# Causal masks of two attention branches moved off TensorE: a kept-at-one scan, GpSimd on the diagonal blocks

## The reference, cut to what matters

```python
# branch A, stick-breaking, strictly causal (s < t)
z = einsum("bhqd,bhkd->bhqk", q, k) * 128 ** -0.5
log_keep = where(mask, log_sigmoid(-z), 0.0)
between = cumsum(log_keep, reverse=True) - log_keep
w = where(mask, exp(log_sigmoid(z) + between), 0.0)
# branch B, forgetting attention, causal (s <= t)
logits = z + cum_q[..., :, None] - cum_k[..., None, :]
p = softmax(where(s <= t, logits, -inf))
```

## Time and profile before

| | |
|---|---|
| median of 3 runs | 3790.38 us (3785.99 to 3910.45) |
| the profiled execution | 3785.02 us |
| its span on the slowest core (core 0) | 3783.5 us |
| spans of the 8 cores | 3759.2 to 3783.5 us |
| branch A, from the first scan to the last product | 107.0 to 595.7 us of the span |
| branch B, from the first addition to the last scaling | 595.7 to 1065.8 us |
| mask products | 256 |

### The profile page before, as it was taken

One profiled execution on the slowest core, in us unless ns is written; L12 is line 12 of the kernel. 1 busy time (PEld: TensorE's weight loads), 2 busy tenths in 40 slices (PEclk: granted clock), 3 DMA queues, 4 the chain that ended last, 5 costly groups with the idle time before them and its releaser, 6 DMA issues.

```text
span 3783.5 us, 56865 instructions; the slowest of 8 cores (3759.2 to 3783.5 us)
## 1 busy us (share of the span) xinstructions
PE 3683.0 (97%) x21124; PEld 1837.0 (49%) x21124; DVE 1738.2 (46%) x1692; ACT 1140.3 (30%) x1796; POOL 348.3 (9%) x467
## 2 busy tenths in 40 slices
PE   7999999999889999999999999999999999999999
PEld 6555656656534444444444444444444444444444
DVE  5788888887833333334333333332222322322233
ACT  5667777877731112222121111110001000000001
POOL 1000000000021112112110000000000000000001
PEclk9999999999999999999999999999999999999999
DMA  7565656767774467778895556556665565455568
GB/s 252 131 151 132 141 139 147 163 156 153 164 214 167 140 200 236 231 239 264 237 263 192 190 193 235 195 182 205 206 198 189 188 223 181 176 206 205 178 221 268
DMA packets 422367, 733.03 MB, mean 194 GB/s; under 512 B 333120, under 2 KB 333504, under 8 KB 352592
## 3 DMA queue, kind: packets, MB, share of 16 engines
q1 hardware_dynamic: 380048, 509.11, 45.1%
q0 software_dynamic: 40896, 216.10, 18.7%
q10 hardware_dynamic: 1152, 4.19, 0.3%
HBM read 567.77 MB, written 81.85 MB: 172 GB/s over the span
## 4 chain that ended last, share of the span: by engine, by line
PE 82%; DVE 7%; DMA 6%; issue 3%; ACT 1%; SPq 0%; POOL 0%; DVEq 0%; ACTq 0%; POOLq 0%
PE ps L78 82%; DVE Pr L78 5%; DMA WT<-W 2%; DMA xb<-x 1%; DVE W L78 1%; DMA OT<-OTs 1%; DMA mixs<-ost 1%; DMA xs<-x 1%; ACT W L78 0%; SPq L78 0%; DVE lg L78 0%; DVE wbf L78 0%; ACT kp L78 0%; DVE hb L78 0%; DVE ost L78 0%
## 5 line engine op out<-in xcount | busy, mean ns | idle before, releaser
L78 PE MATMUL ps<-u2T,wbf 128*128 128x512 bf16 x5632 | 1215.9, 379 | 0.0
L78 PE MATMUL ps<-uT,wbf 128*128 128x512 bf16 (+1 forms) x4480 | 940.6, 363 | 13.1 <-ACT sg L78 6.5
L78 PEld LDWEIGHTS ps<-u2T,wbf 128*128 128x128 bf16 x5632 | 551.1, 98 | 664.5
L78 DVE CAST wbf<-wst 128x2048 bf16<-128x2048 f32 x426 | 528.0, 1264 | 515.3 <-PE ps L78 429.3
L78 PEld LDWEIGHTS ps<-uT,wbf 128*128 128x128 bf16 x4480 | 416.1, 99 | 458.9 <-issue 20.5
L78 PE MATMUL ps<-wbf,aT 128*128 128x512 bf16 x2464 | 532.1, 379 | 0.0
L78 ACT ACTIVATE sg<-ps 128x512 f32<-128x512 f32 x264 | 155.0, 597 | 1234.3 <-PE ps L78 1214.2
L78 DVE TENSOR_TENSOR aT<-ps,sg 128x512 bf16<-128x512 f32 x176 | 121.6, 691 | 762.7 <-PE ps L78 759.7
L78 PEld LDWEIGHTS ps<-wbf,aT 128*128 128x128 bf16 x2464 | 241.1, 98 | 290.7
L78 DVE TENSOR_TENSOR_SCAN Pr<-kp 128x2047 bf16<-128x2047 f32 (+15 forms) x128 | 310.0, 2422 | 34.2 <-ACT kp L78 25.0
L78 ACT ACTIVATE junk<-ps 128x512 bf16<-128x512 f32 x128 | 76.5, 598 | 782.0 <-DVE ost L78 744.0
(11 more groups left out here) (96 smaller groups left out, 2039.9 us busy)
## 6 DMA issues: line engine op xcount, KB each, us to landing
wst<-wfg_t SPq DMA_DIRECT2D x88, 1024.0 KB, 7.3
wst<-wfu_t SPq DMA_DIRECT2D x88, 1024.0 KB, 5.4
wst<-wfd_t SPq DMA_DIRECT2D x88, 1024.0 KB, 5.8
wst<-wg_t SPq DMA_DIRECT2D x56, 1024.0 KB, 8.0
wst<-wqkv_t POOLq DMA_DIRECT2D x42, 1024.0 KB, 7.0
wst<-wo_t SPq DMA_DIRECT2D x32, 1024.0 KB, 7.9
wst<-wb_t SPq DMA_DIRECT2D x30, 1024.0 KB, 8.4
xs<-x SPq DMA_DIRECT2D x16, 1024.0 KB, 11.7
```

The costliest lines, as they stand in the source:

```text
L78: ins = getattr(eng, meth)(**kw)
```

## The change

- The mask product in `Zp` goes, in both branches, and with it the reading of `cbf` by the scores.
- Branch A, the product: the scan becomes state = max(state * kp, U), where `U` is a row pattern (`Um`, bfloat16, 128 x 2048) that is 0 everywhere but in the last 128 columns, and there 1 on the masked elements (s >= t within the block). The factor is below one, so a masked position keeps the state at one. `Um` lies in the memory of the second `Llo` tile, is written once by GpSimd ahead of the heads, and is read with its end laid at the row's end.
- Branch A, the weight: GpSimd multiplies the diagonal block of `W` by a 0/1 tile (`low_bf`), in place, after the sigmoid of the piece that has the block and before VectorE's product.
- Branch B: GpSimd adds `mfx_bf` (0 and -1e30) onto the 128 columns of `Lhi` or `Llo` that belong to the next row's diagonal block, in place (`mask_next`). The call stands behind VectorE's addition of the row's first piece where i > 8 and behind that of its last piece otherwise; after row 0 it is done for row 15 of the next head. The rows come in falling order, so a block that was lowered is not read again in that head.
- The first load of the second `Llo` tile moves from the early part of branch A to the start of branch B, since `Um` lies there.

```diff
@@ _emit @@
-    msb_bf = cbf.t[:, 0:128]
+    low_bf = cbf.t[:, 0:128]
+    upp_bf = cbf.t[:, 384:512]
...
+    Um, Umr = fx["Llo"][1].view([128, S], BF16), fx["Llo"][1].r
+    kb.op(POOL, "memset", dict(ap=Um[:, 0:S - 128], constant=0.0), writes=[Umr])
+    kb.op(POOL, "tensor_copy", dict(out=Um[:, S - 128:S], in_=upp_bf), reads=[cbf.r], writes=[Umr])
...
+    def mask_next(h, i):
+        L = fx["Lhi"] if i >= 8 else fx["Llo"][h % 2]
+        blk = L.t[:, (i % 8) * 128:(i % 8 + 1) * 128]
+        kb.op(POOL, "tensor_tensor", dict(out=blk, in0=blk, in1=mfx_bf, op=ALU.add), reads=[cbf.r], writes=[L.r])
@@ Zp @@
-            dg = e == 128 * (i + 1)
...
-            if dg:
-                calls.append(("matmul", dict(out=t[:, e - 128 - a:e - a], lhsT=ident_bf, rhs=msb_bf if hx < NH else mfx_bf,
-                                             start=False, stop=True, skip_group_check=True)))
-        kb.group(PE, calls, reads=[qT.r, kT.r, cbf.r], writes=rs)
+        kb.group(PE, calls, reads=[qT.r, kT.r], writes=rs)
@@ X_sb @@
+        if b == n:
+            kb.op(POOL, "tensor_tensor", dict(out=w_.t[:, n - 128:n], in0=w_.t[:, n - 128:n], in1=low_bf, op=ALU.mult),
+                  reads=[cbf.r], writes=[wh[1 if a else 0]])
         if last:
             kb.op(DVE, "tensor_tensor_scan", dict(out=Pr.t[:, n - 2::-1], data0=k_.t[:, n - 1:0:-1],
-                                                  data1=k_.t[:, n - 1:0:-1], initial=1.0, op0=ALU.mult, op1=ALU.min),
-                  reads=[k_.r], writes=[Pr.r])
+                                                  data1=Um[:, S - 1:S - n:-1], initial=1.0, op0=ALU.mult, op1=ALU.max),
+                  reads=[k_.r, Umr], writes=[Pr.r])
@@ X_fox @@
+        if a if i > 8 else last:
+            if i:
+                mask_next(h, i - 1)
+            elif h + 1 < NH:
+                mask_next(h + 1, NB - 1)
@@ loop over the pieces @@
         if hx == NH and pieces[g][1] == NB - 1 and pieces[g][2]:
             fox_setup()
+            mask_next(0, NB - 1)
+            loadL(1, 0)
         if g == 30:
             loadL(0, 1)
             loadL(0, 0)
-            loadL(1, 0)
```

More of the change, by code:

```diff
@@ L300, in build_nc @@
     G["bf_d"] = nc.dram_tensor("bfg", [128, 128], F32, kind="ExternalInput").ap()
-    G["cbf_d"] = nc.dram_tensor("cbf", [128, 3 * 128], BF16, kind="ExternalInput").ap()
+    G["cbf_d"] = nc.dram_tensor("cbf", [128, 4 * 128], BF16, kind="ExternalInput").ap()
     G["cf_d"] = nc.dram_tensor("cf32", [128, 4 * 128 + 1], F32, kind="ExternalInput").ap()
@@ L359, in _emit @@
     final_events = []
-    cbf = Slot(kb, "cbf", [128, 3 * 128], BF16, dma=True)
+    cbf = Slot(kb, "cbf", [128, 4 * 128], BF16, dma=True)
     cf = Slot(kb, "cf", [128, 4 * 128 + 1], F32, dma=True)
@@ L1368, in _consts @@
     cb = np.concatenate([
-        np.where(s >= j, -1e30, 0.0),
+        np.where(s < j, 1.0, 0.0),
         np.where(s > j, -1e30, 0.0),
         np.eye(128),
+        np.where(s < j, 0.0, 1.0),
     ], axis=1).astype(ml_dtypes.bfloat16)
```

## The result

The changed kernel takes 3815.87 us (median of 5 runs) against 3785.99 us before in the same set. The ratio, 1.0075 with a 95% interval of [1.0052, 1.0099], leaves out one run before and two of the changed kernel that fell into the chip's slower state. The forecast was 3786 us, no change. The kernel is slower, by about 29 us: clear of the interval, inside the stated range of 3765 to 3826 us, and well under 2%.

What follows compares the result with a forecast made beforehand. TensorE was taken to bound branch B, with TensorE and VectorE both nearly full in branch A. The sum was 3785.0 - 6.3 - 3.6 + 8.4 = 3783.5 us, put at 3786 us as a median, range 3765 to 3826 us.

Steps and rivals of the forecast that it cites:

- TensorE's gain: Dropping 256 mask products at 0.056 us each takes 6.3 us off the path in branch B, 3.6 in branch A.
- Branch A's cost: GpSimd's 128 products on `W` cost VectorE 2.1 us a head; half counts, adding 8.4 us over branch A.
- the two engines shutting each other out: Branch A: GpSimd's masks and VectorE's two-operand work block each other, 0.1 us a row, 1.6 us a head.
- masks late in GpSimd's queue: Branch A: masks behind two weight loads a head come late, VectorE's product waits 0.25 us more each, 0.5 us a head.
- Branch B's cost: GpSimd's 128 additions in branch B make VectorE late at a head's turn but not TensorE; counted as nothing.
- I count nothing: Branch B: VectorE, idle 10 us a head, catches up after waiting for masks, so GpSimd's additions add no time.
- only at the end of a head is there less: Branch B: elsewhere VectorE's own work and waits between additions cover the 0.7 us a mask needs.
- the cover of 0.4 us: Branch B, head's turn: VectorE's late addition still ends 0.4 us before the scores needing its PSUM pair, so TensorE isn't late.
- the second: Rival, branch B: the head's turn starves TensorE, 4 to 14 us, upper rows as much again; about 3800 us, chance 0.14.
- Fixed price: Rival, branch A: each GpSimd mask keeps VectorE out 1.11 us whatever its size; 3891 us, slower by 2.8%, chance 0.05.
- No contention: Rival, branch A: masks fit the gaps or scans don't keep GpSimd out; only gain remains, 3771 to 3775 us, chance 0.22.
- The level: Whole kernel: the median lies 5.4 us above the profiled execution, so the 3783.5 us sum was put at 3786 us.

Runs made afterwards that it cites:

- b_no_lmask: Kernel before with branch B's mask product removed and no GpSimd additions, so its causal mask is left out; six heads of B 342.0 us, the branch 459.3 us.
- d_b: Kernel before, but in branch B GpSimd writes lowered blocks into small tiles three rows ahead and VectorE adds in two operations; ratio 0.9977 to before in both sets.
- ost_act: Changed kernel with the 64 stores of finished outputs issued from ScalarE's queue instead of GpSimd's; ratio to before 1.0100, six heads of branch B 356.1 us.
- only_b: Branch B as changed, branch A as in the kernel before; mean span 3781.5 us against 3760.9 before, from one run, six heads of B 360.5 us.

## Why the prediction was wrong

- *TensorE's gain.* Right in a full head: a mask product was 0.056 us, and branch B without masks runs at 56.63 us a head. Over the whole branch 3 to 5 us came of it, not 6.3 (`b_no_lmask` 459.3 us, `d_b` 457.2, for 462.6). In branch A 492.9 went to 488.1, 4.8 us for a forecast 3.6, but only 2 to 3 against the other runs with the old masks, which is within the scatter of that stage.
- *Branch A's cost.* Both causes were named, their sizes were not right: 11.2 us for the 8.4 of the sum. Of the 8.4, 6.4 were for the two engines shutting each other out (measured 5.2) and 2.0 for masks late in GpSimd's queue (measured 6.0 for waits of all kinds), so this term was taken at a third. The mask takes 0.415 us undisturbed (I had 0.39), the scan does shut GpSimd out, and the heads in the middle of branch A take 61.1 us, just over my 60.5 to 61. The net came out at +6.8 us instead of +4.8, or at about +9 as said above.
- *Branch B's cost.* This is the step that failed: "I count nothing". It rested on "only at the end of a head is there less" time between two additions. I compared the mask with VectorE's own work between them and, in the sum, looked for stores and loads in front of it at the head's turn alone. GpSimd's queue has four stores in each head; one stands before the mask of row 5 and waits for `PV` and ScalarE's copy, and the mask waits with it: VectorE idles 5.1 to 5.6 us there in most heads. At the turn I was right on VectorE (row 0's addition 1.3 us late a head, measured 10.3 us in eight) and wrong on the cover of 0.4 us: it goes, and TensorE waits 8.1 us there in seven heads. For each mask the question was not how long GpSimd needs but when the entry in front of it is released. Forecast for the branch: -6.3 us; found: +22. In six heads alone it is -3.7 without additions and +15.8 with them.
- *The rivals.* The nearest was the second, TensorE starved in branch B, about 3800 us, with 0.14; it put the start at the head's turn, 4 to 14 us, and "up to as much again" in upper rows. TensorE's gaps agree in kind: 8.1 us at the turn, but the larger part, 11.3 us, before the scores of row 3, far below the upper rows. That rival is what happened, and it had the smaller chance. Fixed price is out: 128 columns take 0.415 us, 512 take 1.27. No contention is out by the stretched products and by branch A's loss.
- *The level.* That medians lie up to 5 us above a profiled execution played no part: the whole difference is in the stages.

Three things stay open: why with the stores out of the way the transposing DMAs are late in some heads and not in others (from first score to first score 56.7 us in two heads and 59.0 to 66.5 in five, `ost_act`, core 0), where the DMAs were only seen, not tried; how the 6.0 us of waits in branch A divide between GpSimd's queue and the semaphores; and how the 30 us between `only_b` and `d_b` would divide if the tile of its own and the distance were changed apart.

## What to carry to other kernels

When work moves to an engine that was only a DMA queue, list what stands in front of each piece of it and what releases that; a store that nobody waited for becomes a link between four engines. Look further than the first such stall, too: with the stores gone another wait took over most of it. Made three rows ahead into a tile of its own, GpSimd's result cost nothing here; the same work one row ahead, and in place, cost 30 us. And price GpSimd beside two-operand work of VectorE by the rest of the running instruction, not by its own length.

## What the runs showed of the hardware

A scan on VectorE with both operands in SBUF keeps a GpSimd product of 128 x 128 out for as long as it runs: the product took 0.415 us at least and 3.88 us at most, and none of the 80 that started inside a scan ended inside it, while a memset of the same block took 0.204 to 0.226 us in 125 of 125 cases. A 128 x 2047 scan takes 4.42 us whether its second operand is the same float32 tile or a bfloat16 one.
